# A fused two-block transformer kernel: the second shift and scale are summed by column halves, and the first MLP quarter begins on the first half of its input

## The reference, cut to what matters

```python
sh1, sc1, g1, sh2, sc2, g2 = split(silu(c) @ w_mod + b_mod, 6)      # six rows of 2048
x = x + g1 * rms_norm(fourier_mix(modulate(rms_norm(x, g_0), sh1, sc1)) @ fnet_w, g_1)
h = modulate(rms_norm(x, g_2), sh2, sc2)      # norm * (1 + sc2) + sh2, column by column
x = x + g2 * rms_norm(square(relu(h @ w_mlp_in)) @ w_mlp_out, g_3)  # 2048 -> 8192 -> 2048
```

## Time and profile before

| | us |
|---|---|
| median of three runs | 2172.69 |
| lowest, highest | 2172.11, 2174.6 |
| the profiled execution | 2170.78 |
| its span, first to last instruction | 2169.0 |
| PE busy | 2037.3 (94%) |
| DVE busy | 1267.6 (58%) |
| ACT busy | 1016.3 (47%) |
| HBM read | 459.87 MB, 213 GB/s over the span |

### The profile page before, as it was taken

How to read it: one execution, slowest core, us unless ns; L and a number is a source line. 1 busy time by engine, 2 the same in 40 slices (tenths; PEclk the granted TensorE clock), 3 DMA queues, 4 the chain that set the end, 5 groups by cost and what they waited for, 6 DMA issues and landing times.

```text
span 2169.0 us, 23943 instructions
## 1 busy us (share of the span) xinstructions
PE 2037.3 (94%) x9149; PEld 1666.1 (77%) x9149; DVE 1267.6 (58%) x1194; ACT 1016.3 (47%) x1330; POOL 22.8 (1%) x25
## 2 busy tenths in 40 slices
PE   3897279999999999998999999999999999999997
PEld 1775168888888888887788777788888888888886
DVE  7999986655655454456546556654454454454454
ACT  3332154444544444444555745555444444544543
POOL 0000100000000000000000000000000000000000
PEclk9998579999999999999999999999999999999999
DMA  9999976667665555554545444555555555555552
GB/s 401 410 386 351 353 277 239 242 218 249 237 233 178 188 194 195 176 193 155 163 164 162 152 156 155 173 177 182 187 194 193 175 195 191 189 185 193 188 190 101
DMA packets 193756, 463.03 MB, mean 213 GB/s; under 512 B 7400, under 2 KB 7848, under 8 KB 180752
## 3 DMA queue, kind: packets, MB, share of 16 engines
q1 hardware_dynamic: 191808, 455.11, 60.7%
q0 software_dynamic: 848, 3.70, 0.5%
q10 hardware_dynamic: 1024, 3.20, 0.4%
HBM read 459.87 MB, written 2.10 MB: 213 GB/s over the span
## 4 chain that ended last, share of the span: by engine, by line
PE 82%; DVE 9%; DMA 5%; ACT 2%; issue 2%; ACTq 0%; DVEq 0%
PE ps L421 26%; PE ps L423 26%; PE ps L422 26%; DVE scr L1118 5%; DMA raw<-in_w_mod 2%; DVE w_low L1106 2%; PE ps L470 2%; DMA raw<-in_fnet_w 2%; ACT w_high L797 1%; ACT extra L839 0%; DMA junk<-in_g_out_fox 0%; ACT L1004 0%; PE ps L666 0%; PE ps L667 0%; ACT extra L1003 0%
## 5 line engine op out<-in xcount | busy, mean ns | idle before, releaser
L1106 DVE TENSOR_TENSOR w_low<-raw,w_high 128x1024 fp32r<-128x1024 f32 x672 | 820.4, 1224 | 808.1 <-ACT w_high L797 807.8
L797 ACT ACTIVATE w_high<-raw 128x1024 fp32r<-128x1024 f32 x672 | 708.4, 1059 | 915.8 <-PE ps L423 852.9
L421 PE MATMUL ps<-w_high,h_both 128*128 128x512 f32 x1536 | 611.1, 398 | 9.4 <-DVE w_low L1106 8.3
L423 PE MATMUL ps<-w_high,h_both 128*128 128x512 f32 x1536 | 601.1, 391 | 0.0
L422 PE MATMUL ps<-w_low,h_both 128*128 128x512 f32 x1536 | 600.2, 391 | 0.0
L421 PE MATMUL ps<-w_high,u_high 128*128 128x512 f32 x1152 | 451.0, 392 | 0.3 <-DVE u_low L1505 0.3
L423 PE MATMUL ps<-w_high,u_low 128*128 128x512 f32 x1152 | 448.6, 389 | 0.0
L422 PE MATMUL ps<-w_low,u_high 128*128 128x512 f32 x1152 | 448.4, 389 | 0.0
L421 PEld LDWEIGHTS ps<-w_high,h_both 128*128 128x128 f32 x1536 | 289.9, 189 | 70.8 <-DVE w_low L1106 9.5
L423 PEld LDWEIGHTS ps<-w_high,h_both 128*128 128x128 f32 x1536 | 289.6, 189 | 62.1
L422 PEld LDWEIGHTS ps<-w_low,h_both 128*128 128x128 f32 x1536 | 290.2, 189 | 58.1 <-issue 0.5
(11 more groups left out here) (174 smaller groups left out, 782.7 us busy)
## 6 DMA issues: line engine op xcount, KB each, us to landing
raw<-in_w_mod SPq DMA_DIRECT2D x96, 1024.0 KB, 7.0
raw<-in_w_mlp_in SPq DMA_DIRECT2D x64, 1024.0 KB, 5.6
raw<-in_w_mlp_out SPq DMA_DIRECT2D x64, 1024.0 KB, 5.0
raw<-in_w_up SPq DMA_DIRECT2D x64, 1024.0 KB, 5.4
raw<-in_w_down SPq DMA_DIRECT2D x64, 1024.0 KB, 5.0
raw<-in_w_in SPq DMA_DIRECT2D x48, 1024.0 KB, 5.1
raw<-in_fnet_w SPq DMA_DIRECT2D x16, 1024.0 KB, 7.2
raw<-in_w_out SPq DMA_DIRECT2D x16, 1024.0 KB, 5.0
```

The costliest lines, as they stand in the source:

```text
L421: eng.matmul(dst, ah, wh, start=(k == 0), stop=False)
L423: last = eng.matmul(dst, al, wh, start=False, stop=(k == KT - 1))
L797: eng.activation(w_high[:, h % LEAD, :], raw[:, slot, (h % 2) * 2 * CW:(h % 2 + 1) * 2 * CW], ACT.Copy).then_inc(high_ready, 1)
L1106: eng.tensor_tensor(w_low[:, h % LEAD, :], raw[:, slot, piece], w_high[:, h % LEAD, :].bitcast(f32), ALU.subtract).then_inc(raw_used if h ...
```

## The change

- Shift 2 and scale 2 are each cut into column halves A and B (SH2A, SC2A, SH2B, SC2B). A load is now 256 rows x 1024 columns (4 KB per row, two pieces of rows); eight make one half unit. VectorE takes it in two linked operations of 1024 (`half_tile`, L1282).
- All of SH2A and SC2A come ahead of SH2B and SC2B, and eight MLP chunks (UP) are put between the latter. FRONT now has 104 loads.
- Eight half tiles, the first four of SC2A and of SH2B, go to TensorE (`mod_tile` of PE, L486): four fp32 matmuls of 512 columns each, with silu(c)/128 spread as the stationary operand, after two that bring the bias (L494). Their slots are given back by TensorE (`raw_used_pe`).
- The copies of the mixer's four products go from VectorE to ScalarE, and so do the eight normalizations. VectorE does all updates in one piece.
- The first quarter of MLP1 runs three column blocks over the first half of the inputs (six chunks), then the three over the second half, then the rest as before.
- Four of the eight transposed blocks are copied back to `acc` and scaled later.
- The first two quarters are written out where a loop over two stood, and the eight G2 tiles of the first begin later (MOD_FIRST).

```diff
+FRONT += [(SH2A, 6), (SC2A, 0), (SH2A, 7), (SC2A, 1), (SC2A, 2), (SC2A, 3), (SC2A, 4), (SC2A, 5), (SC2A, 6), (UP, 0),
+          (SC2A, 7), (UP, 1),
+          (SH2B, 0), (SC2B, 0), (SH2B, 1), (SC2B, 1), (UP, 2), (SH2B, 2), (SC2B, 2), (SH2B, 3), (SC2B, 3), (UP, 3),
+          (SH2B, 4), (SC2B, 4), (SH2B, 5), (UP, 4), (SC2B, 5), (SH2B, 6), (SH2B, 7), (UP, 5), (SC2B, 6), (UP, 6),
+          (SC2B, 7), (UP, 7)]
...
+UP_FIRST = 3
+FIRST_ORDER = [(c, hh) for half in range(2) for c in range(UP_FIRST) for hh in range(4 * half, 4 * half + 4)] + \
+              [(c, hh) for c in range(UP_FIRST, 2 * NC) for hh in range(HALVES)]
...
+                before = t.c["raw"] - RAW
+                if before in ON_PE:
+                    eng.wait_ge(raw_used_pe, ON_PE.index(before) + 1)
...
+            def mod_tile(unit, r):
...
+                for k in range(2):
+                    weights = silu_p[:, 2 * r + k:2 * r + k + 1].to_broadcast([P, P])
+                    for j in range(2):
+                        column = k * HALF + j * CW
+                        last = eng.matmul(ps[:, ROW_BANK + j, :], weights, raw[:, n % RAW, column:column + CW],
+                                          start=False, stop=k == 1 and r == ROWS_ON_PE - 1)
+                last.then_inc(raw_used_pe, 1)
...
+            for y, (c, hh) in enumerate(FIRST_ORDER):
...
+                if y == 1:
+                    bias_rows(SH2B)
+                    mod_tile(SH2B, 0)
+                elif y == 3:
+                    mod_tile(SH2B, 1)
+                elif y == 5:
+                    mod_tile(SH2B, 2)
+                    mod_tile(SH2B, 3)
+                elif y == 9:
+                    last_read(SH2B, HALVES - 1)
+                    sum_partitions_to_columns(SH2B, SHIFT_B_BANK)
+                elif y == 11:
+                    last_read(SC2B, HALVES - 1)
+                    sum_partitions_to_columns(SC2B, SUM_B_BANK)
```

More of the change, by code:

```diff
@@ L58 @@
 GATE_ROWS = 10
-SC1, SH1, G1, SH2, SC2, G2, FNET = range(7)
-MOD_COLUMNS = (1, 0, 2, 3, 4, 5)
+SC1, SH1, G1, SH2A, SC2A, SH2B, SC2B, G2, FNET, UP = range(10)
+HALF = D // 2
+MOD_COLUMN = {SC1: D, SH1: 0, G1: 2 * D, SH2A: 3 * D, SC2A: 4 * D, SH2B: 3 * D + HALF, SC2B: 4 * D + HALF, G2: 5 * D}
+MOD_INIT = (SC1, SH1, G1, SH2A, SC2A, G2)
 BEHIND_CHUNK = (1, 1, 2, 1)
 FRONT = [(unit, kk) for unit in (SC1, SH1) for kk in range(KT)]
-LATER = [(unit, kk) for unit in (G1, SH2) for kk in range(KT)]
+LATER = [(G1, kk) for kk in range(KT)] + [(SH2A, r) for r in range(HALVES)]
 FRONT += [LATER.pop(0) for _ in range(2)]
@@ L114, in add, with used @@
         self.c[name] += k
+    def used(self, d=0):
+        n = self.c["raw"] + d
+        return self.at("raw", d - sum(p < n for p in ON_PE))
     def arrived(self):
@@ L305, in mod_tile @@
             def mod_tile(unit, kk):
[L306 to L313, removed]
+                column = MOD_COLUMN[unit]
+                if SH2A <= unit <= SC2B:
+                    load(w_mod[2 * kk * P:2 * (kk + 1) * P, column:column + HALF]
+                         .rearrange("(k p) n -> p k n", p=P), 2)
                 else:
-                    mod_tile(unit, k)
+                    load(w_mod[bass.ds(kk * P, P), column:column + D])
             def mlp_chunk(w1, w2, q, ch):
@@ L402, in _, with half @@
             t = Tally()
-            def half(n, hh, high, low):
+            def half(bank, hh, high, low):
                 slot = t.c["half"] % LEAD
@@ L507, in step @@
                         first(hh)
-                        half(n, hh, high, low)
+                        half(2 * (n % 2), hh, high, low)
                         if t.c["half"] % 2 == 0 and (4 * n + hh // 2) - 2 in mods:
@@ L1327, in _ @@
                     gate(NC - 2)
-                elif behind == 3:
-                    t.add("done", 8)
-                    add_step(None, NC - 1, NC - 1)
-                elif behind == 5:
+                elif n == AT[SH2A, 7]:
+                    t.c["squared"] = 2 * TT * NC
+                    t.c["summed"] = NC
                     gate(NC - 1)
                     mean_square()
-                elif behind == 7:
                     invert()
-                    for i in range(2):
+                    for i in range(TT * NC):
@@ L1367, in _ @@
-            eng.wait_ge(acc_init[5], 16)
-            eng.wait_ge(acc_zero, 1)
-            with t.loop(eng, 0, MOD_LOOPS, low=64, raw=32 + len(MOD_AFTER), t=2 * NC, done=64, squared=TT * NC,
-                        summed=NC) as q:
-                mlp_body(acc, q, MOD_AFTER)
+                    mean_square()
+                    invert()
+                elif n == AT[SC2A, 5]:
+                    mod_columns(SH2A, SHIFT_A_BANK)
+                elif n == AT[UP, 1]:
+                    mod_columns(SC2A, SUM_A_BANK)
+                    split_h(0)
+                    split_h(1)
+                elif n == AT[SC2B, 0]:
+                    split_h(2)
+                    split_h(3)
+                elif n == AT[UP, 6]:
+                    mod_columns(SH2B, SHIFT_B_BANK)
+                elif n == AT[SC2B, 7]:
+                    mod_columns(SC2B, SUM_B_BANK)
+                    for i in range(4, 8):
+                        split_h(i)
```

383 lines of the change are left out of this document (249 added, 134 removed).

## The result

| | us |
|---|---|
| after, median of 5 runs (lowest to highest) | 2180.09 (2179.66 to 2183.28) |
| before, median of 5 runs on the same chip | 2172.11 (2170.45 to 2174.6) |
| ratio, with its 95% interval | 1.0044 (1.0033 to 1.0056) |
| profiled execution after, its span | 2179.66, 2177.8 |

The change makes the kernel slower by 8 us, beyond the 0.2% that a measurement can tell. The forecast was 2175.7 us, "no change" the likeliest. The time lies in the range, but by luck: the 8 us come from a place that the prediction costed at nothing.

A forecast was written before the change was run, and what follows sets the result against it. VectorE and DMA bound the stage from 220 to 290 us, TensorE the rest. Terms -1.9 (front), +2.7 (slow-clock start) and +2.4 (hand-overs) give +3.2, say 3: 2172.7 + 3.0 = 2175.7 us, own range 2171 to 2181, wider range 2158 to 2190.

The forecast's parts named there:

- no change: Whole kernel: time within 0.2% (4.3 us) of before, given chance 0.42, against faster 0.20 and slower 0.38.
- Steps 1 to 3: Front up to MLP1: FNET ends at 208 us, four SC2A tiles on TensorE done at 225, MLP1 starts at 249.
- the walk: Six-step timeline of the front in trace times, ending with TensorE going on at 325.7 us; chance 0.53.
- slow-clock rival: TensorE's tiles run at 1.2 GHz if its clock falls before 213 us: about +21 us, 2197; chance 0.11.
- Step 4: Loads behind 243 us: load 86 waits for TensorE's slot until 262, SyncE stops 19 us, TensorE goes on at 287.5.
- rival of the ring that doesn't stop: Loads 86 to 102 run at DMA's pace from 243 us, TensorE going on at 303: 2153 us; chance 0.17.
- Step 5: Last loads and tiles: VectorE done at 317.3 us, DMA with half-tile loads at 2.7 us at 319; 319 taken.
- rival of dear loads: Half-tile loads cost 3.15 us like chunks instead of 2.7: +5 us, 2180.7; chance 0.19.
- Step 6: Sums, scaling and split take 6.7 us; TensorE goes on at 325.7 us, six chunks done, against 327.6 now: 1.9 won.
- some thirty hand-overs that the walk leaves out: Hand-overs in the front, 0.08 us each, adding 2.4 us to the sum.
- signs that the prediction named: MLP1 start 247 to 252 us, issue gap 15 or more, TensorE idle some 4, second half near 326, rest 3 later.
- the rest follows TensorE: Behind about 330 us only TensorE sets the time; later G2 tiles and unrolled quarters cost nothing.

The follow-up runs named there:

- e2: Changed kernel with 176 satisfied waits (88 instructions) on TensorE's queue near 1012 us, ahead of the second MLP; 2173.35 us, ratio 1.0012.
- e3: Changed kernel with TensorE's four SH2B half tiles one place earlier each and SC2A's column sums in bank 4; 2174.48 us, ratio 1.0019 to before.
- e8: Changed kernel with shift 2's second half (SH2B) wholly on VectorE, none of its half tiles on TensorE; 2160.56 us, ratio 0.9955 to before.
- e1: Kernel before with 256 satisfied waits (128 instructions) on TensorE's queue near 1012 us, ahead of the second MLP; 2176.05 us, ratio 1.0027.
- e6: Kernel before with 322 satisfied waits (161 instructions) near the start of TensorE's queue; 2180.71 us, ratio 1.0049.
- e4: Changed kernel with both the earlier half tiles of e3 and the 176 waits of e2; 2163.21 us, ratio 0.9966 to before.
- e7: Kernel before with 338 satisfied waits (169 instructions) near the start of TensorE's queue; 2189.48 us, ratio 1.0084.
- e9: Changed kernel with all eight of TensorE's half tiles on VectorE instead; 2169.18 us, ratio 0.9991 to before.
- e5: As e4, but the 176 satisfied waits stand near the start of TensorE's queue; 2161.07 us, ratio 0.9959 to before.
- e10: e8 with 334 satisfied waits (167 instructions) near the start of TensorE's queue, loops placed as before; 2159.41 us, ratio 0.9944 to before.

## Why the prediction was right and wrong, by its steps

- **Steps 1 to 3** (FNET's end, four tiles beside VectorE, MLP1's start) hold in their order. FNET ended at 204.4 us (206.2 in e2, the same front), not at 208. Predicted start 249, measured 246.9 (248.6 in e2). TensorE's four tiles ran at 2.4 GHz: the 32 records of L486 between 206 and 222 us take 14.2 us, the walk had 13.8. The slow-clock rival didn't occur there, and the rule of the Trainium skill ("TensorE: Matmul & The Clock Gate", Loop structure matters more than you think) by which waits for DMA between the groups let the array go cold held only in part: from 220 to 290 us the mean granted clock is 0.80, with the lower level from 227.8 to 251.7 us and behind the wait that ends at 286.4, but the chunks and tiles from 252 to 282 us ran at the upper.
- **Step 4** (the ring turns against it) holds nearly to the number: a stop of 19 us forecast, 18.8 measured; load 86 at 262, measured 260.4; TensorE goes on at 287.5, measured 286.4. e3 and e8 confirm the mechanism by taking it away. The rival of the ring that doesn't stop gave that a price of 22.7 us; e8 recovers 11.4 of it, with VectorE doing that work again.
- **Step 5** (half-tile loads at 2.7 us, last tile at 319) comes out near, at 317.1, by prices that were too high. A chunk's 3.15 us rests on a miscount: from 107.66 to 132.77 us SyncE issues ten loads, not nine, and five of them are chunks. Behind the first, a chunk, come:

```profile
110.12 2.60 SPq L299 DMA_DIRECT2D raw<-in_w_mod  x2
114.84 0.38 SPq L299 DMA_DIRECT2D raw<-in_fnet_w  x1
117.50 0.33 SPq L299 DMA_DIRECT2D raw<-in_w_mod  x1
119.95 0.38 SPq L299 DMA_DIRECT2D raw<-in_fnet_w  x1
122.40 0.33 SPq L299 DMA_DIRECT2D raw<-in_w_mod  x1
125.13 0.38 SPq L299 DMA_DIRECT2D raw<-in_fnet_w  x1
127.59 0.33 SPq L299 DMA_DIRECT2D raw<-in_w_mod  x1
130.31 0.38 SPq L299 DMA_DIRECT2D raw<-in_fnet_w  x1
```

That is 2.51 us per load by the issues, and 2.67 by the bytes (393 GB/s from 112 to 137 us, 1.05 MB each), so 2.5 to 2.85 for a chunk. In after the full DMA engines (share 1.03) move 392 GB/s from 288 to 320 us, 2.68 us per load in a mix of both kinds. Eleven loads then take 29.4 us instead of 31, and the step ends with VectorE, for which the prediction had 317.3. The rival of dear loads did not occur; that its 2180.7 lies beside the measured 2180.1 is chance. The Trainium skill's rule of one line rate from 512 bytes on ("DMA: Bandwidth & Descriptors", Specifications), by which the prediction got the same 317.3, is nearer to these rows than the prediction's prices. The distance of 2.70 us between half tiles in e8's row ((5.78 - 0.37) / 2) need not be the price of a load: VectorE takes 2.68 for a half tile there (8.03 / 3), and the slots come back from it.
- **Step 6** comes out in its main row and fails in a small term. TensorE goes on at 325.35 (325.7 forecast; 327.34 in e2), by two errors that cancel: step 5 was 1.9 us too long, and from the last tile's sum to TensorE's matmul it is 8.2 us, not 6.7. But "some thirty hand-overs that the walk leaves out", +2.4 us, are not there. In TensorE's order of time, before has its six chunks done at this transposition:

```profile
328.95 0.60 PE L470 MATMUL ps<-cst,scr 128*128 128x128 f32 x4
```

So after is 3.6 us ahead where it goes on; the start at the lower level (until 330.2 us) takes 2.4 back (2.7 forecast), and a transposition that after has still to make 0.5. That is -0.7 us, as measured at the 34 halves, instead of +3: the 1.9 won were 3.6, and the 2.4 of the hand-overs were nothing. (e2 against e1, the same two fronts, gives -0.1: the front is worth nothing to within some 2 us.) Of the signs that the prediction named, the start, the stop, the wait ahead of the seventh half chunk (4.6 us) and the second half came, the start 0.1 us outside its bound. "Everything behind it some 3 us later" did not.
- **What failed is the sentence behind the sum, "the rest follows TensorE"**, with its cover for the unrolled quarter: it was costed at nothing, with TensorE full and VectorE idle as the cover. The cover that mattered was that of instruction fetch, and it was a matter of eight matmuls. e2 takes 8.7 us out of the second MLP, and 7 us out of the time, by shifting the loop alone; e6 makes the kernel before as slow as after (ratio 1.0049) by a shift to the same place.

So the sum that would have been right is -0.7 + 0.7 (the lead is lost at the first MLP's jump) + 8.8 = +8.8 in the spans; the medians show 8.0. The forecast's +3 was 5 us too low, and owed its sign to a term that did not exist. The likeliest case, no change, would have been right for the front.

Open are the 1.0 us of the second MLP that neither gaps nor clock explain, why the clock fell behind one gap of 2 us and not behind the two others, and why TensorE stands still for 0.5 to 1.2 us right at the first MLP's jump in seven of the traces (after, e2, e3, e4, e6, e7, e9) and not in the others. How many pages TensorE keeps wasn't tried beyond seven (kept) and eight (fetched again), both by the count of instructions.

## What to carry to other kernels

Where a change adds or takes instructions ahead of a hardware loop that nearly fills what its engine keeps, compare the loop's duration and the instruction queue's packets in both traces before anything else; gaps "by issue" a few matmuls behind each jump are the sign, and a few satisfied waits placed in idle time move it away. Work given to an idle engine must give its buffer back before that engine has something better to do: four half tiles gained 6 to 7 us ahead of the first chunk, and four others lost 11 between the chunks. Judge the two effects apart, since here each hid the other's size.

## What the runs showed of the hardware

- A loop of 1684 instructions on TensorE is kept over its repetitions when it lies over seven pages by the count (before, e2, e4, e5, e9, e10: no packet on queue 8 from 1615 to 2150 us), and fetched again, 25 to 27 pages in three repetitions, when it lies over eight (after, e1, e3, e6, e7, e8). A page that is fetched again is there 3.75 to 4.55 us behind the jump (after, e3, e6 and e7, three jumps each), so the loss is that less what is left in the first page: 0 with 24 matmuls (e1), 1.7 to 2.1 us with 8 (after, e6), 2.7 to 3.5 with 4 (e7).
- Gaps of 1.7 to 2.4 us were followed by a clock at the lower level in three cases of nine (after, e3, e6, one each), gaps of 2.7 to 3.5 us in three of three (e7: 13.6 us of low clock in all, 6.8 lost).
- Satisfied waits on TensorE aren't free where they stand on its path: 256 of them held it for 9.8 us (an estimate of 38 ns each), against 5.2 us of idle time that was there anyway; 176 at the same place held it for 5.6.
